# Late products of w_ada and the copies of rotated keys and queries, moved to GpSimd

## What is computed

```
c_act = silu(c)
ada = c_act @ w_ada + b_ada                 # 1024 x 6144, six parts of 1024
sh_m, sc_m, g_m, sh_f, sc_f, g_f = split(ada, 6)
h = rmsnorm(x, norm_mix_g) * (1 + sc_m) + sh_m
x = x + g_m * mixer(h)                      # 8 MLA heads and 8 forgetting heads
h = rmsnorm(x, norm_ffn_g) * (1 + sc_f) + sh_f
x = x + g_f * conv_ffn(h)
```

```
q_mla = concatenate([q_nope, q_rope])
k_mla = concatenate([k_nope, broadcast(k_rope, 8 heads)])
```

## Time and profile before

| | |
|---|---|
| time, median of 3 runs | 1063.24 us (1062.43 to 1063.27) |
| the profiled execution | 1060.27 us |
| its span, first to last instruction | 1058.5 us |
| TensorE / VectorE / ScalarE / GpSimd busy | 97% / 65% / 55% / 0% |
| mean granted clock of TensorE | 0.983 |
| HBM read | 194 MB, 184 GB/s over the span |

### The profile page before, as it was taken

How to read it: one execution, slowest core, us unless ns; L and a number is a source line. 1 busy time by engine, 2 the same in 40 slices (tenths; PEclk the granted TensorE clock), 3 DMA queues, 4 the chain that set the end, 5 groups by cost and what they waited for, 6 DMA issues and landing times.

```text
span 1058.5 us, 19761 instructions
## 1 busy us (share of the span) xinstructions
PE 1029.9 (97%) x8306; PEld 992.0 (94%) x8306; DVE 684.4 (65%) x1143; ACT 586.4 (55%) x965; POOL 0.4 (0%) x5
## 2 busy tenths in 40 slices
PE   8999999999999999999999999999999999999996
PEld 4699799989999999899899999999989899999996
DVE  7586777858887676877727654545766557554542
ACT  4679755646555555667736444444666556444442
POOL 0000000000000000000000000000000000000000
PEclk8999999999999999999989999999999999999998
DMA  9665656543666444453314654554544327455511
GB/s 383 276 259 209 230 229 235 215 155 146 227 265 233 165 182 177 159 204 131 145 41 159 242 197 176 183 192 169 228 172 152 125 81 275 165 197 176 182 41 40
DMA packets 27879, 196.40 MB, mean 186 GB/s; under 512 B 3088, under 2 KB 3728, under 8 KB 4496
## 3 DMA queue, kind: packets, MB, share of 16 engines
q1 hardware_dynamic: 26928, 194.16, 49.4%
q10 hardware_dynamic: 864, 0.98, 0.3%
HBM read 194.09 MB, written 1.05 MB: 184 GB/s over the span
## 4 chain that ended last, share of the span: by engine, by line
PE 82%; ACT 8%; DVE 7%; issue 2%; DMA 1%; SPq 0%; DVEq 0%; ACTq 0%
PE PS L835 21%; PE PS L836 20%; PE PS L837 20%; PE PS L958 3%; PE PS L961 3%; PE PS L959 3%; DVE wlo L1514 3%; ACT whi L1179 2%; PE PS L992 1%; PE PS L1112 1%; PE PS L994 1%; PE PS L993 1%; DMA raw<-wada 1%; PE PS L1101 1%; PE PS L1134 1%
## 5 line engine op out<-in xcount | busy, mean ns | idle before, releaser
L1514 DVE TENSOR_TENSOR wlo<-raw,whi 128x1024 fp32r<-128x1024 f32 (+1 forms) x314 | 367.5, 1217 | 131.8 <-ACT whi L1179 131.6
L1179 ACT ACTIVATE whi<-raw 128x1024 fp32r<-128x1024 f32 (+1 forms) x314 | 311.8, 1046 | 172.6 <-PE PS L837 172.6
L835 PE MATMUL PS<-Hh,whi 128*128 128x256 f32 x1200 | 342.5, 285 | 0.7 <-ACT V L1351 0.7
L836 PE MATMUL PS<-Hl,whi 128*128 128x256 f32 x1200 | 339.5, 283 | 0.0
L837 PE MATMUL PS<-Hh,wlo 128*128 128x256 f32 x1200 | 339.5, 283 | 0.0
L835 PEld LDWEIGHTS PS<-Hh,whi 128*128 128x128 f32 x1200 | 230.2, 192 | 4.4 <-issue 2.8
L835 PE MATMUL PS<-Oh,whi 128*128 128x256 f32 x816 | 231.3, 284 | 0.8 <-DVE Ol L1494 0.7
L836 PE MATMUL PS<-Ol,whi 128*128 128x256 f32 x816 | 230.9, 283 | 0.0
L837 PE MATMUL PS<-Oh,wlo 128*128 128x256 f32 x816 | 230.9, 283 | 0.0
L836 PEld LDWEIGHTS PS<-Hl,whi 128*128 128x128 f32 x1200 | 230.3, 192 | 0.1
L837 PEld LDWEIGHTS PS<-Hh,wlo 128*128 128x128 f32 x1200 | 230.2, 192 | 0.0
(11 more groups left out here) (234 smaller groups left out, 1203.7 us busy)
## 6 DMA issues: line engine op xcount, KB each, us to landing
raw<-wall SPq DMA_DIRECT2D x155, 1024.0 KB, 4.9
raw<-wada SPq DMA_DIRECT2D x18, 1024.0 KB, 5.0
GA<-wada SPq DMA_DIRECT2D x2, 1024.0 KB, 26.5
GA<-alibi SPq DMA_DIRECT2D x1, 2048.0 KB, 10.5
raw<-wall SPq DMA_DIRECT2D x2, 768.0 KB, 6.5
X<-xt SPq DMA_DIRECT2D x1, 1024.0 KB, 5.3
KM<-wada SPq DMA_DIRECT2D x1, 1024.0 KB, 16.1
QF<-wada SPq DMA_DIRECT2D x1, 1024.0 KB, 19.6
```

The costliest lines, as they stand in the source:

```text
L835: e.matmul(dst, wh, a, start=start, stop=False, skip_group_check=share)
L836: e.matmul(dst, wh, b, start=False, stop=False, skip_group_check=share)
L1179: e.activation(whi[place(n)][:, c], raw[i % RAW][:, c], ACT.Copy).then_inc(*up("a_whi", (n, half)))
L1514: e.tensor_tensor(wlo[place(n)][:, c], raw[i % RAW][:, c], f32(whi[place(n)][:, c]), ALU.subtract).then_inc(*up("v_wlo", (n, half)))
```

## The change

POOL walks the list of steps too. It takes the step "ada": for k = 0 a scaling of the raw tile into `ACC`, for the other 28 tiles a scaling in place in the `raw` buffer (L835 of the changed kernel) and then an addition into `ACC` (L838), where DVE had one instruction. It takes "copy_key" (L843) and "copy_rope" (L850) from ACT. Each instruction of POOL waits on the semaphore of the one before it. The first scaling of a block waits for TensorE's sum of the block before, and the very first for `v_gs` 3, which DVE raises when the first part of the product is done. Whoever waited for `v_ada`, `a_kr` or `a_qr` waits for `g_ada`, `g_kr` or `g_qr` now. The program of the others is otherwise as it was.

```diff
@@ -784,7 +784,7 @@
                 if was[0] == "w":
                     on.wait_ge("v_wlo", (was[1], 1))
                 else:
-                    on.wait_ge("v_ada", ("late", was[1], 2 * was[2] + 1))
+                    on.wait_ge("g_ada", ("late", was[1], 2 * was[2] + 1))
             if it[0] == "ada":
                 e.dma_start(raw[slot][:, :], wada[it[1] * 4 + it[2]]).then_inc(*up(f"d_raw{slot}", i, 16))
             else:
@@ -813,7 +813,42 @@
         e.wait_ge(marks.sems["d_out"], 64)
 
     def gpsimd(e):
+        on = On(e, marks)
         e.memset(ONES[:, :], 1.0).then_inc(*up("g_ones", 0))
+        begun = ("g_ones", 0)
+        for step, *a in STEPS:
+            if step == "ada":
+                i, cb, kk = a
+                on.wait_ge(f"d_raw{i % RAW}", i)
+                for half in range(2):
+                    k = 2 * kk + half
+                    slab = raw[i % RAW][:, half * 1024:(half + 1) * 1024]
+                    on.wait_ge(*begun)
+                    if k == 0:
+                        on.wait_ge("a_c", 0)
+                        if cb > 2:
+                            on.wait_ge("t_ada", ("late", cb - 1))
+                        else:
+                            on.wait_ge("v_gs", 3)
+                        e.tensor_scalar(ACC[:, :], slab, CA[:, 0:1], None, ALU.mult).then_inc(*up("g_ada", ("late", cb, k)))
+                    else:
+                        e.tensor_scalar(slab, slab, CA[:, k:k + 1], None, ALU.mult).then_inc(
+                            *up("g_ada", ("scaled", cb, k)))
+                        on.wait_ge("g_ada", ("scaled", cb, k))
+                        e.tensor_tensor(ACC[:, :], ACC[:, :], slab, ALU.add).then_inc(*up("g_ada", ("late", cb, k)))
+                    begun = ("g_ada", ("late", cb, k))
+            elif step == "copy_key":
+                on.wait_ge(*begun)
+                on.wait_ge("v_kr", "turned")
+                e.tensor_copy(KM[64:96, :, :], V[64:96, 0, 256:512].unsqueeze(1).to_broadcast([32, 8, T])).then_inc(
+                    *up("g_kr", 0))
+                begun = ("g_kr", 0)
+            elif step == "copy_rope":
+                on.wait_ge("v_qr", "sum")
+                for j in range(4):
+                    on.wait_ge(*begun)
+                    e.tensor_copy(QM[64:96, j:8:4, :], TT[32 * j:32 * j + 32, :, :]).then_inc(*up("g_qr", j))
+                    begun = ("g_qr", j)
 
     def tensor(e):
         on = On(e, marks)
@@ -935,7 +970,7 @@
                 free[6 + p % 2] = ("v_adab", ("first", p))
             elif step == "ada_sum":
                 cb, b = a
-                on.wait_ge("v_ada", ("late", cb, 7))
+                on.wait_ge("g_ada", ("late", cb, 7))
                 bank(b)
                 for j in range(8):
                     m = e.matmul(
@@ -1089,8 +1124,8 @@
                         h = 2 * i + j
                         q, k = QM[0:96, h, :], KM[0:96, h, :]
                         on.wait_ge("a_ev", (NUMBER[("uq", 0)], 1))
-                        on.wait_ge("a_qr", 0)
-                        on.wait_ge("a_kr", 0)
+                        on.wait_ge("g_qr", 3)
+                        on.wait_ge("g_kr", 0)
                         on.wait_ge("a_ev", (NUMBER[("ukv", 0)], 1))
                     else:
                         q, k = QM[64 * j:64 * j + 64, i, :], KM[64 * j:64 * j + 64, i, :]
@@ -1327,16 +1362,7 @@
                 e.activation(
                     KF[64:80, :, :], PTf[0:16, 1024:1280].unsqueeze(1).to_broadcast([16, 8, T]), ACT.Copy).then_inc(
                     *up("a_f", "keys"))
-            elif step == "copy_key":
-                on.wait_ge("v_kr", "turned")
-                e.activation(
-                    KM[64:96, :, :], V[64:96, 0, 256:512].unsqueeze(1).to_broadcast([32, 8, T]), ACT.Copy).then_inc(
-                    *up("a_kr", 0))
             elif step == "copy_rope":
-                on.wait_ge("v_qr", "sum")
-                for j in range(4):
-                    m = e.activation(QM[64:96, j:8:4, :], TT[32 * j:32 * j + 32, :, :], ACT.Copy)
-                m.then_inc(*up("a_qr", 0))
                 sq_free[0] = sq_free[1] = ("v_qr", "sum")
             elif step == "ev_vf":
                 n, b, j = a
@@ -1542,21 +1568,6 @@
                 e.scalar_tensor_tensor(
                     GS[:, 2 * p:2 * p + 2], ADA[:, 8 + 2 * p:10 + 2 * p], 1.0, col("norm_mix_g", 2 * p, 2),
                     ALU.add, ALU.mult).then_inc(*up("v_gs", p))
-            elif step == "ada":
-                i, cb, kk = a
-                for half in range(2):
-                    k = 2 * kk + half
-                    src = raw[i % RAW][:, half * 1024:(half + 1) * 1024]
-                    on.wait_ge(f"d_raw{i % RAW}", i)
-                    if k == 0:
-                        on.wait_ge("a_c", 0)
-                        if cb > 2:
-                            on.wait_ge("t_ada", ("late", cb - 1))
-                        e.tensor_scalar(ACC[:, :], src, CA[:, 0:1], None, ALU.mult).then_inc(*up("v_ada", ("late", cb, k)))
-                    else:
-                        on.wait_ge("v_ada", ("late", cb, k - 1))
-                        e.scalar_tensor_tensor(ACC[:, :], src, CA[:, k:k + 1], ACC[:, :], ALU.mult, ALU.add).then_inc(
-                            *up("v_ada", ("late", cb, k)))
             elif step == "ada_sum":
                 cb, b = a
                 on.wait_ge("t_ada", ("late", cb))
@@ -1740,7 +1751,7 @@
                 if pr == 1:
                     on.wait_ge("v_qr", 1)
                     e.tensor_tensor(TT[:, :, :], TT[:, :, :], SQ[:, 0:2, :], ALU.add).then_inc(*up("v_qr", "sum"))
-                    tt_free[0] = tt_free[1] = ("a_qr", 0)
+                    tt_free[0] = tt_free[1] = ("g_qr", 3)
             elif step == "gated":
                 n, i, b0, b1 = a
                 gm, gf = pair(GA, 2 * i), pair(GA, 8 + 2 * i)
```

## The result

The changed kernel takes 1081.72 us (median of 4 runs, 1078.89 to 1083.25) against 1063.18 for the kernel before (4 runs): a ratio of 1.0177 [1.0158, 1.0197], 18.5 us slower. The profiled execution took 1083.25 us, with a span of 1081.4. One execution of all those reported here was left out, 1289.77 us at a mean granted clock of 0.713, of the kernel in which POOL only adds.

What follows compares the result with a forecast made beforehand. TensorE, busy 97% of the span, was taken as the bound. Profiled 1060.27 + 4 + 1.8 + 0.9 + 3 - 3.6 = 1066.4; with the runs' median 3.0 above that execution, 1069.3 us, range 1059 to 1082.

Steps and rivals of the forecast that it cites:

- the price of POOL's scaling: One POOL pass over 1024 columns: taken at 1.0 us, between 0.75 and 1.9, from POOL's fills.
- The slot comes free about as early as before: POOL's head start and 6.4 us a load free load slots on time, except some 2 us late at each block's first.
- POOL itself too slow: Rival, chance 0.10: 12.8 us a load, block 4 done at 204, TensorE's sum 8 us late; 1072 to 1078 us.
- Contention: DVE standing while POOL works on SBUF, taken nearer to full exclusion than none: 4 + 1.8 + 0.9 + 3 us.
- The reciprocals: DVE's reciprocals of the norms at 68.67 us come 0 to 8 us late: 4 us of TensorE pause, 1.8 for clock.
- The last mixer tile: DVE's low part at 45.52 us may wait behind a POOL addition: 0 to 2.3 us, taken as 0.9.
- The probabilities' scalings: DVE's four scalings per head, 116 to 187 us, pass their 3.2 us cover: 0 to 12.6 us, taken as 3.
- The gain: TensorE wins the 1.9 us pause near 109 us and 1.7 us of clock: 3.6, from 7.7 us off the chain.
- The 0.7 us at L1351 stay: TensorE's 0.7 us wait on L1351 remains, because that evacuation follows TensorE's own matmuls of the same bank.
- the clock's 1.7 us: From 112 to 116.3 us the clock is 0.60 behind the pause; at 1.00 this would save 1.7 us.
- The copies wanted late: Copies wait behind POOL's fourth load, but are wanted only at 115.2 us by L1351 and near 138.3 by MLA scores.
- The feed-forward stretch at nothing: From 264 to 320 us contention costs 0, since the weights have chunks in hand that cover DVE's waits.

## Why the prediction was off

The forecast was 6 us slower, and it was 18.5. The sign held; the time lies inside the range by 0.3 us, and that is luck, since the range's upper end was made of contention and the loss is mostly lateness. The size did not hold, and the mechanism was the one that was given 0.10.

- **What bounds the kernel** held: POOL's exclusion with DVE showed up only where TensorE waits.
- **The step that failed is the price of POOL's scaling**, taken at 1.0 us from the fills of constants, with 1.9 as its upper end. It takes 2.85, and 3.43 in the mean. The addition was right (2.2; measured 2.34 to 2.42). So a half costs about 6 us instead of 3.2, and all the products 182 us (96.1 + 72.5 + 13.6) instead of 94; the upper end was 139. A fill reads nothing and a copy runs at 1.1 ns a column, so neither was near an arithmetic form; the rows could not say that, and the range should not have stopped at two passes.
- **"The slot comes free about as early as before"** rested on 6.4 us a load, and with it lateness stood at nothing in the sum. At 11 to 14.5 us it fell: SP waited 123 us for POOL, against 71 for DVE before, and lateness cost 16 us. With the scalings left out, 5.5 us a load, both long pauses are gone.
- **The rival, POOL itself too slow,** named the right engine and the right stretch, but not the right wait. It had block 4 done at 204 and TensorE's sum of it 8 us late; the block was done at 210.5, and no one waited for that sum. What TensorE waited for there was SP's issue of weights behind the third load (199.5), which the rival names second. It assumed 12.8 us a load and added 3 to 9 us. The prediction's last sign of being wrong, time lost in slots with SP waiting for POOL and ACT for DMA, is what the trace shows. The rival missed two things: block 3 was late too (5.2 us of pause at 159), and each pause costs twice, once by itself and once by the slow clock behind it.
- **Contention** was put at 9.7 us in the sum (4 + 1.8 + 0.9 + 3) and measured 5.9, within its bounds. Its places were mostly wrong. The reciprocals came at 69.05 and cost no wait (in the kernel that only adds they did, 3.2 us). The last mixer tile cost nothing: DVE's part of it comes 0.4 us later than before, but TensorE stands 0.4 later already at 42.99, ahead of POOL's first product (44.06). The probabilities' scalings did rise to 833 ns from 285, but TensorE waited 0.2 us for them. The keys' evacuation near 90 us, 1.3 us here and 3.7 where POOL's work is waited for by nobody, was not in the list. The chain leads from it back to 75.35 us, where a scan of DVE (L1730) takes 2.78 us beside an addition, against 0.68 before.
- **The gain** of 3.6 us was measured at 3.2, for another reason than given. "The 0.7 us at L1351 stay" was wrong: where the pause at 109 goes, the wait at L1351 grows to 2.3 us (with one load on POOL), since that evacuation follows ACT's own chain. Nor were the clock's 1.7 us there to be won: with only the copies on POOL the clock is 1.00 from 112 to 116.3, and TensorE still goes on at 116.12 instead of 116.35. What pays is that this whole chain comes 2.1 us earlier. That the copies "stand on the chain", 2.5 us, was true of the trace, and worth nothing alone.
- **The copies wanted late** held: `KM` was filled at 102.0 and `QM` at 112.0, and nobody waited. **The feed-forward stretch at nothing** is within what could be measured.

## What to carry to other kernels

An idle engine is not free: before work is moved to it, put a price from a row of the same operation on it, or run the operation once, and then ask by when the result is due in each place, not what the total is. Here DVE's 1.28 us became 5.3 to 6, which was nearly harmless in the block where loads lay far apart (+1.5 us) and cost 16 us where eight lay close together and held the load queue. And when two branches meet, move a little of both: one load of sixteen and five copies beat the kernel, each of them alone did nothing, and all of it lost 18.5 us. The gain of the small version is 0.3%.

## What the runs showed of the hardware

POOL's scaling of 128 x 1024 float32 takes 2.85 us, a product with a broadcast column 1.96 and a copy 1.12: the scaling reads one tile, as the copy does, and is the slowest of all. The slow form is the kinder neighbour, since it holds DVE for 0.98 us and then lets it run beside (2.35 us for 2.36), and the faster one doesn't.

The same program can meet a lower clock in one execution and not in the next. The kernels with one load and with one load and the last block are the same up to 264 us; from 62 to 69 us, in windows as above, TensorE was granted 0.76 in the first and 1.00 in the second:

```profile
62.00:69.00 7.00, 7.00 (x48) 7.00 (x49) 4.90 (x6) 6.36 (x8) 0.00 (x0) 0.76 0.97 354
```

```profile
62.00:69.00 7.00, 6.63 (x55) 6.43 (x55) 4.74 (x7) 6.91 (x10) 0.00 (x0) 1.00 0.82 308
```

At 97 us the first is 1.6 us behind the second, and its span is 1.9 us longer. The changed kernel has the same 0.76 there, and it is not POOL's doing: POOL is idle there in the first of these two, and with only the products on POOL, at work for 6.90 of these 7 us, the clock is 1.00. A single profile of this kernel can't tell a gain of 2 us.
